# Attention by pairs of heads, projection pieces at the mLSTM's gates, and squares taken once x is there

## What is computed

```python
for layer in range(2):
    mod = silu(c) @ w_ada + b_ada               # shift, scale, gate; x has one c, the context another
    h = rms_norm(x) * (1 + scale) + shift
    aq, ak, av, mq, mk, mv, mo, mg, pp = split(h @ w_in)
    att = softmax(q k' / 8) v                   # 8 heads of 64, 2 key heads; latent rows see 512 keys,
                                                # context rows 256
    ml  = mlstm both ways (mq, mk, mv, gates mg), normed, * sigmoid(mo)
    pool = banded means of pp, mixed by pool_w
    x = x + gate1 * (concat(att, ml, pool) @ w_out)
    x = x + gate2 * swiglu(h2)
```

## Time and profile before

| | us |
|---|---|
| three timed runs, median (lowest, highest) | 2075.32 (2073.78, 2077.52) |
| the profiled execution | 2075.85 |
| its span, first to last instruction | 2074.0 |
| TensorE busy in the span | 1943.3 |
| VectorE, ScalarE, GpSimd busy | 1094.1, 758.6, 112.5 |
| mean granted TensorE clock | 0.968 of full |

### The profile page before, as it was taken

How to read it: one execution, slowest core, us unless ns; L and a number is a source line. 1 busy time by engine, 2 the same in 40 slices (tenths; PEclk the granted TensorE clock), 3 DMA queues, 4 the chain that set the end, 5 groups by cost and what they waited for, 6 DMA issues and landing times.

```text
span 2074.0 us, 34392 instructions
## 1 busy us (share of the span) xinstructions
PE 1943.3 (94%) x15100; PEld 1657.1 (80%) x15100; DVE 1094.1 (53%) x1685; ACT 758.6 (37%) x1059; POOL 112.5 (5%) x120
## 2 busy tenths in 40 slices
PE   5899999899999997899899999999998999989998
PEld 2666657577787786676899999998987777789997
DVE  1734464533333326555655466645766676467654
ACT  2423354322122214335433444343444343344332
POOL 0011001000000010010000100002001111000000
PEclk9889999999999999898999999999999999999999
DMA  8233302355245421210455555553441110245552
GB/s 308 102 132 133 121 21 89 115 183 183 92 146 181 160 73 51 72 42 22 164 184 183 176 197 186 181 183 122 158 150 59 43 43 27 78 157 177 183 176 82
DMA packets 37157, 266.22 MB, mean 128 GB/s; under 512 B 4112, under 2 KB 4112, under 8 KB 6672
## 3 DMA queue, kind: packets, MB, share of 16 engines
q1 hardware_dynamic: 36720, 260.87, 36.2%
q10 hardware_dynamic: 288, 3.15, 0.4%
HBM read 262.96 MB, written 1.05 MB: 127 GB/s over the span
## 4 chain that ended last, share of the span: by engine, by line
PE 85%; DVE 9%; ACT 3%; issue 1%; DMA 1%; SPq 0%; DVEq 0%; ACTq 0%
PE ps L579 20%; PE ps L581 19%; PE ps L580 19%; PE ps L2620 2%; PE ps L909 2%; DVE W L559 2%; PE ps L1249 2%; PE ps L1227 2%; PE ps L1453 1%; PE ps L585 1%; PE ps L1466 1%; PE ps L587 1%; PE ps L586 1%; PE ps L1238 1%; PE ps L920 1%
## 5 line engine op out<-in xcount | busy, mean ns | idle before, releaser
L559 DVE TENSOR_TENSOR W<-ring,W 128x2048 fp32r<-128x2048 f32 (+2 forms) x194 | 430.9, 2222 | 283.9 <-ACT W L550 283.7
L550 ACT ACTIVATE W<-ring 128x2048 fp32r<-128x2048 f32 (+2 forms) x194 | 359.1, 1853 | 127.1 <-PE ps L581 120.0
L579 PE MATMUL ps<-h_lat,W 128*128 128x256 f32 x1056 | 301.8, 286 | 4.1 <-DVE h_lat L734 4.0
L580 PE MATMUL ps<-h_lat,W 128*128 128x256 f32 x1056 | 299.8, 284 | 0.0
L581 PE MATMUL ps<-h_lat,W 128*128 128x256 f32 x1056 | 299.7, 284 | 0.0
L579 PEld LDWEIGHTS ps<-h_lat,W 128*128 128x128 f32 x1056 | 203.5, 193 | 5.6 <-issue 4.8
L580 PEld LDWEIGHTS ps<-h_lat,W 128*128 128x128 f32 x1056 | 203.9, 193 | 0.3 <-issue 0.2
L581 PEld LDWEIGHTS ps<-h_lat,W 128*128 128x128 f32 x1056 | 203.7, 193 | 0.0
L579 PE MATMUL ps<-hidden_lat,W 128*128 128x256 f32 x528 | 150.4, 285 | 6.6 <-DVE hidden_lat L895 6.6
L892 DVE TENSOR_TENSOR work<-work,ps 128x256 f32<-128x256 f32 (+1 forms) x88 | 43.0, 488 | 212.1 <-ACT work L867 212.0
L581 PE MATMUL ps<-hidden_lat,W 128*128 128x256 f32 x528 | 150.2, 284 | 0.0
(11 more groups left out here) (365 smaller groups left out, 4079.2 us busy)
## 6 DMA issues: line engine op xcount, KB each, us to landing
ring<-w_up_dram SPq DMA_DIRECT2D x88, 1024.0 KB, 4.9
ring<-w_ada_dram SPq DMA_DIRECT2D x48, 1024.0 KB, 4.9
ring<-w_down_dram SPq DMA_DIRECT2D x43, 1024.0 KB, 4.9
ring<-w_rkv_dram SPq DMA_DIRECT2D x13, 1024.0 KB, 5.0
ring<-w_fm_dram SPq DMA_DIRECT2D x10, 1024.0 KB, 4.9
ring<-w_out_dram SPq DMA_DIRECT2D x8, 1024.0 KB, 4.9
ring<-w_gates_dram SPq DMA_DIRECT2D x8, 1024.0 KB, 4.9
ring<-w_qk_dram SPq DMA_DIRECT2D x6, 1024.0 KB, 4.9
```

What stands on the lines that cost most here:

```text
L550: act.activation(slots[SLOT[s]][:, 0, 0:cols], ring[:, u % RING, 0:cols], ACT.Copy).then_inc(w_high, 1)
L559: dve.tensor_tensor(slots[SLOT[s]][:, 1, 0:cols], ring[:, u % RING, 0:cols], slots[SLOT[s]][:, 0, 0:cols], ALU.subtract).then_inc(w_low, 1)
L579: pe.matmul(o, slots[SLOT[s]][:, 0, at:at + cols], high, start=first, stop=False)
L580: pe.matmul(o, slots[SLOT[s]][:, 0, at:at + cols], low, start=False, stop=False)
```

## The change

- The fold's constant moves to the common ones. SP loads `par`, ada unit 0, the common constants, x, and then units 1 and on; block 1's table goes as a transfer of its own ahead of unit 11, with a semaphore `first_in`, on which TensorE, VectorE and GpSimd wait at the mLSTM.
- x's squares are no longer spread over the eight ada units: ScalarE makes them in iterations 2, 3 and 4, GpSimd adds seven of them up (`pool_sums`, six additions), and TensorE sums in two matmuls behind iteration 6. `act_root` stands ahead of the last `take_ada`.
- `EARLY` = 2 pieces of `FILL` are done ahead of step 0. In layer 0 one stands ahead of each of the first two running maxima, in layer 1 both stand between the projections and the gates' columns. ScalarE's high split of the third fm unit stands ahead of the gates, VectorE's low split behind its |f|; VectorE's split of the fourth stands behind the first weights of the mLSTM.
- Attention has two heads (b = 0 and 1) per turn: scores of both, then values of both, key tile by key tile in turns, of the pair two turns back, then the transposes of both of the pair one turn back. Scores have four banks, `probs` and `probsT` four buffers each, outputs two banks. ScalarE and VectorE keep their order by head.

```diff
+EARLY = 2
 def fill_steps(l, n):
-    return range(n * len(FILL[l]) // STEPS, (n + 1) * len(FILL[l]) // STEPS)
+    rest = len(FILL[l]) - EARLY
+    return range(EARLY + n * rest // STEPS, EARLY + (n + 1) * rest // STEPS)
...
         def act_ada(act):
-            act.wait_ge(x_in, 16)
             for x in range(ADA_FIRST):
-                act_square(act, 0, x)
+                if x == 2:
+                    act.wait_ge(x_in, 16)
+                for m in {2: (0, 1, 2), 3: (3, 4), 4: (5, 6, 7)}.get(x, ()):
+                    act_square(act, 0, m)
+                if x == ADA_FIRST - 1:
+                    act_root_ready(act)
+                    act_root(act, 0)
                 take_ada(act, x, 4 + 2 * (x % 2))
...
+            if layer == DEPTH - 1:
+                pe.wait_ge(ml_abs, layer + 1)
+                for x in range(EARLY):
+                    pe_fill(pe, layer, x)
             pe_gate_columns(pe, layer)
...
-            split(eng, s0 + 2)
+            split(eng, s0 + 2 + (me == 0))
             gate_rows(eng, layer)
-            split(eng, s0 + 3)
...
-            split(eng, s0 + 4)
+            if me == 0:
+                split(eng, s0 + 4)
...
+            if layer == 0:
+                pe_fill(pe, 0, 0)
+            pe.wait_ge(first_in, 16)
             running_max(0, 0)
+            if layer == 0:
+                pe_fill(pe, 0, 1)
             running_max(0, 1)
...
+            if layer == DEPTH - 1:
+                act_fill_pieces(act, layer, range(EARLY))
             act.wait_ge(ml_cols, layer + 1)
...
             take_running_max(0, 0)
+            if layer == 0:
+                act_fill_pieces(act, 0, range(EARLY))
             take_running_max(0, 1)
...
             dve.scalar_tensor_tensor(out=ml_e1, in0=lf, scalar=-1.0, in1=lf, op0=ALU.mult, op1=ALU.max).then_inc(ml_abs, 1)
+            dve_split(dve, FIRST_OF_KIND[f"fm{layer}"] + FILL_FROM + 1)
             dve.wait_ge(ml_ln, layer + 1)
...
             log_weights(0)
+            dve_split(dve, FIRST_OF_KIND[f"fm{layer}"] + FILL_FROM + 2)
...
+            for i in range(n + 2):
+                if i == 1:
+                    pe.wait_ge(pl_low, layer + 1)
                 if i < n:
+                    if i >= 2:
+                        pe.wait_ge(at_exp, base + 2 * i - 2)
+                    for x in (2 * i, 2 * i + 1):
+                        qt, j, b, nk = units[x]
+                        pe.matmul(ps[:, score_bank(x), 0:nk], proj[64 * b:64 * b + 64, AQ + j, qt * P:(qt + 1) * P],
+                                  proj[64 * b:64 * b + 64, AK, 0:nk], start=True, stop=True).then_inc(at_s, 1)
...
+                if i >= 2:
+                    p = i - 2
+                    nk = units[2 * p][3]
+                    pe.wait_ge(at_pt, base + 2 * p + 2)
...
                     for s in range(nk // P):
+                        for b in range(2):
+                            mm = pe.matmul(ps[64 * b:64 * b + 64, p % 2, 0:P], tm[:, s, AV + 64 * b:AV + 64 * b + 64],
+                                           probsT[(2 * p + b) % 4][:, s * P:(s + 1) * P], start=(s == 0), stop=(s == nk // P - 1),
+                                           skip_group_check=True)
...
+                if 1 <= i <= n:
+                    for x in (2 * i - 2, 2 * i - 1):
+                        pe.wait_ge(at_p, base + x + 1)
+                        if x >= 2:
+                            pe.wait_ge(at_pt, base + x - 1)
+                        for s in range(units[x][3] // P):
+                            mm = pe.transpose(ps[:, 6 + x % 2, s * P:(s + 1) * P], probs[x % 4][:, s * P:(s + 1) * P], K("ident"))
...
-            pool.wait_ge(const_in, 16)
+            pool_sums(pool, 0)
+            pool.wait_ge(first_in, 16)
...
-            sp.dma_start(const[:, 0:COMMON_N + ONE_N], dram["const"]).then_inc(const_in, 16)
-            load_unit(sp, 1)
+            sp.dma_start(const[:, 0:COMMON_N], dram["const"][:, 0:COMMON_N]).then_inc(const_in, 16)
             sp.dma_start(xT[:, :, :].rearrange("p k t -> p (k t)"), dram["x"]).then_inc(x_in, 16)
-            for u in range(2, len(UNITS)):
+            for u in range(1, len(UNITS)):
+                if u == RAW_UNITS[ADA_FIRST - 1] + 4:
+                    sp.dma_start(const[:, COMMON_N:COMMON_N + ONE_N], dram["const"][:, COMMON_N:COMMON_N + ONE_N]).then_inc(first_in, 16)
                 load_unit(sp, u)
```

More of the change, by code:

```diff
@@ L214 @@
 FILL = [fill_pieces(l) for l in range(DEPTH)]
+EARLY = 2
 def fill_steps(l, n):
-    return range(n * len(FILL[l]) // STEPS, (n + 1) * len(FILL[l]) // STEPS)
+    rest = len(FILL[l]) - EARLY
+    return range(EARLY + n * rest // STEPS, EARLY + (n + 1) * rest // STEPS)
 def step_of(l, x):
-    return next(n for n in range(STEPS) if x in fill_steps(l, n))
+    return -1 if x < EARLY else next(n for n in range(STEPS) if x in fill_steps(l, n))
 def fill_last_step(l, phase, i):
@@ L407 @@
 ADDS = KT - 2
-SUMS_DONE = [KT + sum(x is not None for x in SUMS[1:r + 1]) for r in range(len(SUMS))]
+SUMS_DONE = [sum(x is not None for x in SUMS[:r + 1]) for r in range(len(SUMS))]
 class Chain:
@@ L504, in build @@
         tm = work[:, TM_AT:H_IN].rearrange("p (k c) -> p k c", c=TM)
-        par_in, const_in, x_in, second_in, lora2_in = (sem(f"{x}_in") for x in ("par", "const", "x", "second", "lora2"))
+        par_in, const_in, first_in, x_in, second_in, lora2_in = (sem(f"{x}_in") for x in ("par", "const", "first", "x", "second", "lora2"))
         loaded = [sem(f"loaded{j}") for j in range(RING)]
@@ L1077, in act_fill, with act_fill_pieces @@
         def act_fill(act, layer, step):
-            for x in fill_steps(layer, step):
+            act_fill_pieces(act, layer, fill_steps(layer, step))
+        def act_fill_pieces(act, layer, pieces):
+            for x in pieces:
                 phase, i, m, k0, k1, at, done = FILL[layer][x]
@@ L1240, in pe_attention @@
-                if i >= 3:
-                    x = i - 3
-                    qt, j, b, nk = units[x]
-                    pe.wait_ge(at_pt, base + x + 1)
-                    if x == 2:
-                        pe.wait_ge(ml_mixed, layer + 1)
-                    if x >= 6 and b == 0:
-                        pe.wait_ge(at_out, (base + x) // 2 - 2)
-                    for s in range(nk // P):
-                        mm = pe.matmul(ps[64 * b:64 * b + 64, (x // 2) % 3, 0:P], tm[:, s, AV + 64 * b:AV + 64 * b + 64],
-                                       probsT[x % 2][:, s * P:(s + 1) * P], start=(s == 0), stop=(s == nk // P - 1),
-                                       skip_group_check=True)
-                    mm.then_inc(at_o, 1)
@@ L1387, in build @@
         gated, pooled = nb[:, 0], nb[:, 1]
-        probs = [ebuf[:, 0, 0], ebuf[:, 0, 1], ebuf[:, 1, 0]]
-        probsT = [ebuf[:, 1, 1], proj[:, MK]]
+        probs = [ebuf[:, b, d] for b in range(2) for d in range(2)]
+        probsT = [hnum[:, d].rearrange("p t h v -> p (t h v)")[:, b * TA:(b + 1) * TA] for d in range(2) for b in range(2)]
         at_small = proj[:, MK + 1, 0:4 * 64].rearrange("p (k n) -> p k n", k=4)
```

90 lines of the change are left out of this document (39 added, 51 removed).

## The result

The changed kernel takes 2040.24 us (median of 4 runs, 2039.42 to 2047.18), the kernel before 2075.36 beside it: ratio 0.983, 95% interval 0.9811 to 0.9849, a gain of 35.1 us. The forecast was 2017 with a range up to 2037, so it was wrong by 23 us, and the range by 3. The profiled execution took 2039.42 (span 2037.4).

A forecast was written before the change was run, and what follows sets the result against it. TensorE was taken as the bound, carrying 85% of the chain of waits. Gains of 9.5 (start), 9.3 and 11.1 (gates) and 28.9 (attention) sum to 58.8 us, from 2075.85 to 2017 us, range 2003 to 2037.

The forecast's parts named there:

- Layer 1's gates: Layer 1's gates and sixteen mLSTM steps: earlier scores 4.9, pieces 5.5, clock 2.2, less 1.5, a gain of 11.1 us.
- VectorE's columns now wait for ScalarE ... 835.9 and not 839.0: Layer 1's gates: columns come at 835.9, so maxima start 3.0 us earlier and scores 4.9 us earlier.
- the lower level ... is another 2.2: Behind layer 1's first mLSTM score: the lower clock level, which lasted 4.5 us more, is another 2.2 us gained.
- Layer 0's gates: Layer 0's gates and mLSTM steps: scores 1.6 us earlier, pieces 5.5, clock 2.7, less 0.5 for bubbles, gain 9.3 us.
- Start: Before the first projection: earlier loads and fewer square sums end the sums at 32.2, not 41.7, gain 9.5 us (7 to 11.6).
- Attention: Attention of both layers: head pairs share the array, wide pairs 3.8 us for 5.32, narrow 2.45 for 3.15, gain 28.9 us.
- Rival (b): Start and gates give half, held by the loads or ScalarE's order: 15 us less, 2032 us; chance 0.18.
- (a): Attention: the clock stays down from the split on, making pairs slower, 2038 us; chance 0.13.
- (c): Attention: the array halves don't overlap in a row of pairs, wide pairs stay 5.3 us, 2047 us; chance 0.06.
- (d): Attention, better than forecast: wide pairs 3.4 us and no fall of the clock, 2006 us; chance 0.12.
- (e): Attention, slower: each pair runs alone, 6.9 us per wide pair and 4.65 per narrow, 2085 us; chance 0.03.
- The lower bound for the gates: Gates of both layers together: at least 12 us gained, if ScalarE becomes the bound with the clock as now; upper bound 24.

The follow-up runs named there:

- e13: Changed kernel with layer 1's first token-major weight unit in slot 2, plus 24 unread 128x256 matmuls in each of layer 1's steps 0 and 8: 2044.74 us.
- e9: Changed kernel with unread 128x384 matmuls at the start, four between products 0 and 1, one behind each of products 1 to 5: 2043.13 us.
- e12: Changed kernel with layer 1's first token-major unit in slot 2, plus unread matmuls, eight behind its gate columns, four behind the first running maximum: 2040.71 us.

## Why the prediction was wrong

- **Layer 1's gates, 11.1 predicted, -2.4 measured.** Two steps of it failed. "VectorE's columns now wait for ScalarE ... 835.9 and not 839.0" took ScalarE to be free: I moved its split ahead of the exponential without asking what the split itself waits for. That cost 4.8 us, and mending it gave 6.45 there. The first score came 1.4 us later after the gate rows (29.56 to 30.96) and not 4.9 sooner: 6.3 of the 13.5 us. And "the lower level ... is another 2.2", with the two pieces' 5.5 taken as pure gain: the pieces were the dense work of the steps. The half level did not shrink by 4.5 us but grew by 12.2 there, and the steps took 1.0 us longer where the terms say 6.2 shorter: the other 7.2. e13 put a price on it.
- **Layer 0's gates, 9.3 and 7.9.** The chain held: first score 1.27 us sooner after the gate rows (1.6 predicted), and 6.6 of the 8.2 for pieces and clock. That the 6.6 is so near is in part luck: the changed steps scatter over 9.6 us between executions, and by the middle traces the whole is 6.3.
- **Start, 9.5 and 7.8** (6.9 at the reciprocal). The loads came as worked out (product 1 at 14.19), the adds were done in time. Mis-sized was the rate: products every 2.8 us, not 2.7, and both sums at the half rate; I took 32.2 for their end, the middle of my bounds (30.1 and 34.3), and it was 34.9, outside them. e9 shows that the rate is what set this.
- **Attention, 28.9 and 24.6.** Pairs share the array, and the wide (3.78) and narrow (2.49) periods were right, as was the stall (3.89 for 4.1). Behind it layer 0 had the half level for 6.8 us where I had 3.4 (1.7 us), and the pairs ahead of the split took 4.50, 4.31 and 3.90 (1.3 us). The rest, 1.3, I leave to fill and drain; no row was set against it. In layer 1 the half level behind the split fell from 13.7 us to 3.4, as predicted.
- **Rivals.** Rival (b), start and gates by half, 2032, was the nearest in kind: they gave 13.3 of 29.9, 16.6 less than forecast and not 15, and the attention another 4.3 less. (a)'s 2038 is nearest in number, but by luck: the attentions had 6.8 and 3.4 us at the half level, and the steady pairs none. (c), (d) and (e) are out by the pair's period of 3.78 us. (The sum for (e) is 67 us and not 68, which changes nothing.)
- The range left no room for a part that turns negative. The lower bound for the gates (12 of 12 to 24) had the clock "as now" for its worst case; they gave 5.5.

What stays open: why the clock falls where it does, at a bare step 6 or 15 as at 0 and 8, can't be told from these rows, and the total's share of each part is known to 2 or 3 us only.

## What to carry to other kernels

Before a split, a copy or a load is moved ahead of something urgent, ask what it waits for at the new place, in each layer by itself: the slot it takes may be held by work that runs later. Ask it again of the mend: the slot that freed layer 1's gates held up the end of layer 0. Where dense matmuls stand between narrow ones, price their removal with the granted clock of that stretch: here taking out 5.6 us of them gained 1.8 to 3.6. When repeats differ by more than the effect, judge by the stages in the traces, and by all of them: a stage that wins can have its price in one that the edit was not meant to touch. Only what comes out differently in traces of the same instructions is scatter.

## What the runs showed of the hardware

- Repeats of one kernel differ by up to 12 us (e9: 2034.16 to 2046.29), and the mean granted clock tells why: 0.971 for the fastest, 0.965 for the slowest. Over all 88 runs of the changed kernel and the experiments' kernels, each taken around its own kernel's mean, a thousandth of mean clock goes with 1.4 us, and what is left scatters by 1.2 us. In some stages the half-level stretches lie differently in each execution: layer 0's sixteen steps took 135.9 to 145.4 us for the same instructions. In others they repeat: layer 1's gate rows to its attention took 115.0 to 115.1 us in five traces, with 17.1 us at the half level at the same place each time.
- TensorE was busy but for 0.11 us and stayed at 1.2 GHz for 16.9 us (start), and fell to it without a pause of its own (e12). What it did then was matmuls of 32 and 2 columns, or of 4 and 64 rows.
- Values of two heads on either half of the columns take 1.09 us for 16 records, scores on either half of the rows 1.13 for four, and changing between them within a pair cost nothing that the rows show.
